# Moving the second group's memory rows and x to later places in the DMA queue of a two-group encoder kernel

## The reference, cut to what matters

```python
def memory_attention(q, mem, mem_norm, w_mem_kv, q_norm, k_norm):
    q = rmsnorm(q.reshape(B, S, MEM_HEADS, MEM_HEAD_DIM), q_norm)
    kv = rmsnorm(mem, mem_norm) @ w_mem_kv      # needs the mean square of each row of mem
    ...
def trunk(x, mem, p):
    for i in range(DEPTH):                      # 2 layers
        h = rmsnorm(x, p['norm_in'][i])
        z = h @ (a_w_in or b_w_in)              # q parts, q_mem, gate
        mix = mla_mixer(...) if i % 2 == 0 else swa_mixer(...)
        mem_o = memory_attention(q_mem, mem, ...)
        branch = concatenate([mix, mem_o]) * silu(gate)
        x = x + branch @ p['w_out'][i]
    return x
y_prompt, y_sample = trunk(x_prompt, mem_prompt, p), trunk(x_sample, mem_sample, p)
```

## Time and profile before

| | before |
|---|---|
| median of three runs | 1411.21 us |
| profiled execution | 1412.02 us, its span 1410.2 us |
| TensorE (PE) busy | 1383.9 us, 98% |
| VectorE (DVE) busy | 972.9 us, 69% |
| ScalarE (ACT) busy | 759.3 us, 54% |
| GpSimd (POOL) busy | 408.4 us, 29% |
| moved by DMA | 122.52 MB, mean 87 GB/s |

### The profile page before, as it was taken

One profiled execution on the slowest core, in us unless ns is written; L12 is line 12 of the kernel. 1 busy time (PEld: TensorE's weight loads), 2 busy tenths in 40 slices (PEclk: granted clock), 3 DMA queues, 4 the chain that ended last, 5 costly groups with the idle time before them and its releaser, 6 DMA issues.

```text
span 1410.2 us, 22918 instructions
## 1 busy us (share of the span) xinstructions
PE 1383.9 (98%) x8072; PEld 1233.9 (87%) x8072; DVE 972.9 (69%) x2035; ACT 759.3 (54%) x1815; POOL 408.4 (29%) x525
## 2 busy tenths in 40 slices
PE   7899999999999999999999999999999999999999
PEld 5688989888888889899888898898888888899997
DVE  6356578888674646898664656878876556488883
ACT  6344466556463535777453544665555445377661
POOL 2032243321021302655212212423302022238450
PEclk9999999999999999999999999999999999999999
DMA  5422221111542132221454132211123412222222
GB/s 212 143 56 73 79 85 44 49 48 35 193 148 79 50 101 78 69 70 56 135 164 131 46 90 79 68 47 44 50 91 115 138 57 71 76 87 68 68 76 105
DMA packets 89825, 122.52 MB, mean 87 GB/s; under 512 B 10480, under 2 KB 58992, under 8 KB 89712
## 3 DMA queue, kind: packets, MB, share of 16 engines
q1 hardware_dynamic: 84240, 113.36, 26.3%
q10 hardware_dynamic: 5472, 7.69, 1.8%
HBM read 116.82 MB, written 4.19 MB: 86 GB/s over the span
## 4 chain that ended last, share of the span: by engine, by line
PE 86%; DVE 5%; ACT 3%; POOL 2%; DMA 2%; issue 2%; SPq 1%; ACTq 0%; DVEq 0%; POOLq 0%
PE bank L1577 25%; PE bank L1579 24%; PE bank L1578 24%; PE bank L1623 8%; PE bank L1583 2%; PE bank L1584 2%; DVE w_lo_t L932 1%; POOL rr L1399 1%; DMA w_raw<-in_w_out 1%; DMA w_raw<-in_w_a 1%; POOL rtmp L1398 1%; ACT w_hi L579 1%; DVE ss L952 1%; ACT q_st L601 0%; DVE cT L942 0%
## 5 line engine op out<-in xcount | busy, mean ns | idle before, releaser
L932 DVE TENSOR_TENSOR w_lo_t<-w_raw,w_hi 128x256 fp32r<-128x256 f32 (+3 forms) x540 | 305.2, 580 | 266.0 <-ACT w_hi L579 252.8
L579 ACT ACTIVATE w_hi<-w_raw 128x256 fp32r<-128x256 f32 (+3 forms) x544 | 268.2, 508 | 336.2 <-PE bank L1579 302.5
L1577 PE MATMUL bank<-w_hi,actT 128*128 128x256 f32 (+3 forms) x1120 | 362.1, 323 | 7.8 <-DVE w_lo_t L932 7.8
L1578 PE MATMUL bank<-w_lo_t,actT 128*128 128x256 f32 (+3 forms) x1120 | 360.0, 321 | 0.0
L1577 PEld LDWEIGHTS bank<-w_hi,actT 128*128 128x128 f32 x1120 | 213.0, 190 | 24.2 <-issue 5.8
L1578 PEld LDWEIGHTS bank<-w_lo_t,actT 128*128 128x128 f32 x1120 | 213.1, 190 | 14.6
L1460 POOL TENSOR_TENSOR prob<-prob,rinv 128x256 f32<-128x256 f32 x192 | 136.4, 740 | 257.6 <-DVE rinv L1038 257.6
L604 ACT ACTIVATE prob<-bank,nmax 128x256 f32<-128x256 f32 (+2 forms) x256 | 138.7, 552 | 106.1 <-DVE nmax L1242 39.7
L1579 PE MATMUL bank<-w_hi,brlo 128*128 128x256 f32 (+1 forms) x608 | 188.9, 311 | 0.0
L1579 PE MATMUL bank<-w_hi,actT 128*128 128x512 f32 (+3 forms) x512 | 170.8, 334 | 0.0
L1577 PE MATMUL bank<-actT,w_hi 128*128 128x512 f32 x384 | 152.5, 397 | 0.0
(11 more groups left out here) (151 smaller groups left out, 2682.7 us busy)
## 6 DMA issues: line engine op xcount, KB each, us to landing
w_raw<-in_w_mem SPq DMA_DIRECT2D x64, 256.0 KB, 2.7
w_raw<-in_w_out SPq DMA_DIRECT2D x112, 128.0 KB, 2.1
w_raw<-in_w_b SPq DMA_DIRECT2D x112, 128.0 KB, 2.1
w_raw<-in_w_b SPq DMA_DIRECT2D x48, 256.0 KB, 2.7
w_raw<-in_w_out SPq DMA_DIRECT2D x40, 256.0 KB, 2.7
w_raw<-in_w_a SPq DMA_DIRECT2D x32, 256.0 KB, 2.7
w_raw<-in_w_a SPq DMA_DIRECT2D x64, 128.0 KB, 2.0
bias<-in_alibi ACTq DMA_DIRECT2D x28, 192.0 KB, 2.3
```

Of the source, the lines that this page charges most:

```text
L579: act.activation(w_hi[:, n % SPLIT, 0:width], w_raw[:, n % RAW, 0:width], ACT.Copy).then_inc(w_hi_done, 1)
L932: dve.tensor_tensor(w_lo_t[:, n % SPLIT, 0:width], w_raw[:, n % RAW, 0:width], w_hi[:, n % SPLIT, 0:width].bitcast(fp32), ALU.subtract).th ...
L1577: nc.tensor.matmul(out, lhs[0], rhs[0], start=start, stop=False, skip_group_check=skip)
L1578: nc.tensor.matmul(out, lhs[0], rhs[1], start=False, stop=False, skip_group_check=skip)
```

## The change

The rows of the second group's memory are no longer loaded ahead of tile 16. They are loaded at the end of layer 0, where x of that group was. `last_squares` and `memory_scales(1)` run in layer 1 instead of layer 0. x of the second group is loaded in layer 1, between tile 163 (the last of `qmem`) and tile 164 (the first of `gate` 8 to 11), still behind the wait on `ssm_ready`.

```diff
@@ block.sync
-                for j in range(NM):
-                    sp.dma_start(last_rows[:, j, :], mem[GROUPS - 1, j * P:(j + 1) * P, :]).then_inc(last_rows_in[j], 16)
                 at = FIRST["qmem", 0, NT - 1]
                 for L in range(LAYERS):
+                    if L % 2 == 1 and L // 2 + 1 < GROUPS:
+                        load_weights(at, FIRST["gate", L, 11])
+                        at = FIRST["gate", L, 11]
+                        load_x(L // 2 + 1)
                     if L + 1 < LAYERS:
                         load_weights(at, FIRST["out", L, 0, NT - 1])
                         at = FIRST["out", L, 0, NT - 1]
                         load_mem(L + 1)
-                    if L % 2 == 0 and L // 2 + 1 < GROUPS:
-                        load_x(L // 2 + 1)
+                    if L == 0:
+                        for j in range(NM):
+                            sp.dma_start(last_rows[:, j, :], mem[GROUPS - 1, j * P:(j + 1) * P, :]).then_inc(last_rows_in[j], 16)
@@ block.scalar
-                    if L == 0:
+                    if L == 1:
                         last_squares()
@@ block.gpsimd
                     batches(MH, MD, NT)
+                    if L == 1:
+                        memory_scales(1)
                     if L == 0:
-                        memory_scales(1)
```

## The result

The changed kernel takes 1400.87 us (median of four runs, 1400.37 to 1402.63), the kernel before 1410.95 us on the same chip: ratio 0.9933, 95% interval 0.9916 to 0.9950, so 7 to 12 us less. Run again later beside the other kernels it took 1401.53 us against 1409.32, ratio 0.9947 (0.9934 to 0.9960). The forecast was 1405.0 with a range of 1401.5 to 1409.5: the direction was right, the gain was larger than forecast and just outside the range.

A forecast was written before the change was run, and what follows sets the result against it. TensorE, busy 98% of the span, was taken as the bound, so only its stalls or low-clock stretches could be given back. -2.6 - 2.3 - 1.3 = -6.2 us gave 1405.0 us against the median, range 1401.5 to 1409.5.

The forecast's parts named there:

- rival F: Further on in the kernel: another wait takes the gain back, counted as no change; chance 0.04.
- Part 3: Layer 1: x ahead of tile 164, the rows' squares and the scales cost 0, with up to 1.4 us kept open.
- rival E: Layer 1: x's 2.1 MB ahead of tile 164 stalls TensorE, net +6.9 us, 1418.1; chance 0.05.
- Part 1: Start of layer 0: without the rows ahead, tile 16's pause falls from 5.4 to 2.75 us, -2.6, and the clock holds, -2.3.
- The clock's term: Behind tile 16's pause in layer 0: TensorE's clock stays at full speed after the shorter pause, -2.3 us.
- rival C: Layer 0: tile 16 lands in time, pause and low clock both go, -9.0 us in all, 1402.2; chance 0.18.
- Rival D: Layer 0: the tables, not the rows, hold the queue ahead of tile 16; only -2.3 us, 1408.9; chance 0.13.
- The rows' term: Ahead of tile 16 in layer 0: removing 1.05 MB of rows at 400 GB/s saves 2.6 us.
- The term of 1.3 at tile 132: End of layer 0, output projection: waits of 1.15 and 0.18 us go, gain 1.3 us, between 0 and 1.3.

The follow-up runs named there:

- x_ahead_of_qmem: Changed kernel with the second group's x issued ahead of tile 156, layer 1's first `qmem` tile, and rows squared earlier: 1411.83 us, ratio 1.0011 to the kernel before.
- rows_stay_tables_later: Kernel before with only the five tables moved from ahead of tile 16 to behind tile 19, rows staying: 1404.69 us against 1409.86, ratio 0.9961.
- rows_behind_16: Kernel before with the two row DMAs issued directly behind tile 16 instead of ahead of it: 1405.23 us against 1410.07, ratio 0.9968.
- tables_behind_19: Changed kernel with the five table loads moved from ahead of tile 16 to behind tile 19: 1400.91 us, ratio 0.9942 to the kernel before.
- rows_eighth: Kernel before with rows moved between tiles 23 and 24, except one eighth (two 64 KB DMAs) left ahead of tile 16: 1403.09 us against 1410.07.
- before_busy_wait: Kernel before with 40 identity transposes on TensorE ahead of its wait for tile 16: 1407.32 us against 1409.86, ratio 0.9982.

## Why the prediction was wrong in size

**The plan of the argument held.** TensorE's waits were the right place to look; the three that the change touches went or shrank to 0.54 us, and nothing took their place (rival F). ScalarE's squares, GpSimd's scales and x in layer 1 cost nothing, as in Part 3. x_ahead_of_qmem shows that rival E was a real danger: x did not stop TensorE ahead of `gate`, where a tile lasts 2.7 us, and did ahead of `qmem`, behind tiles of 1.4 us. Its price was put at 13.1; one chunk earlier, and with the wait for the squares in it, it was 9.0.

**The step that failed** is in Part 1: "I count the issue time at nothing" and "the tile then lands at 45.64 - 2.6 = 43.0". The rows were sized by their bytes alone at 400 GB/s. Measured, the tile lands 4.8 us earlier, not 2.6, so the pause went from 5.37 to 0.54 us and not to 2.75. These are the landings, counted in the kernel before from this line:

```profile
32.34 0.33 SPq L536
```

| ahead of tile 16 | its issue after tile 15's, us | its DMA, us | landing after tile 15's issue, us | TensorE's wait, us |
|---|---|---|---|---|
| tables and rows (before) | 3.69 | 9.61 | 45.64 - 32.34 = 13.3 | 5.37 |
| rows (rows_stay_tables_later) | 2.57 | 6.27 | 41.30 - 32.46 = 8.8 | 0.91 |
| tables (after) | 2.75 | 5.75 | 38.95 - 30.45 = 8.5 | 0.54 |
| tables, rows behind (rows_behind_16) | 2.75 | 6.34 | 41.11 - 32.02 = 9.1 | 1.17 |
| neither (tables_behind_19) | 2.58 | 2.8 | 37.54 - 32.15 = 5.4 | none |

Each line is one profile. With the tables alone the landing is 7.9 to 8.9 us in five of them, with both 12.9 to 13.3 in three, so 4.8 is good to about half a microsecond. The wait is the landing less 7.9 to 8.0 us in each line that has one: by then the tile must be there. Tables alone add 3.1 us, rows alone 3.4, both 7.9, more than their sum. The rows thus cost more behind the tables (4.8) than alone (3.4), and both more than 1.05 / 0.4 = 2.6.

The second and third column say where the sum goes wrong. From its own issue the tile takes 3.0 us longer behind the tables, 3.5 behind the rows and 6.8 behind both, which is nearly the sum. The rest is the issue: tile 16's ring place comes free only 2.6 us after tile 15's issue, and in that time the issues of the tables or those of the rows fit, but not both. So the issues of one of the two cost nothing, and those of the other come on top.
The 4.8 us are thus 0.95 us of earlier issue and 3.9 us of a shorter DMA, and both parts were sized wrong. But it can't be said that issue time as such costs 0.95: rows_eighth has the two issues as well and lands at 8.3. What the profile shows beside it is the start of the stream: with the whole rows in the queue it begins later, 18 GB/s at 36 to 38 us in the earlier trace rows against 95 GB/s already at 34 to 36 us after, 1.9 us being the shift between the two. I had seen the dead time and taken it as given by the tables. Why the stream starts later with the rows in the queue, and why 1.05 MB take over 3 us where 400 GB/s would need 2.6, stays open; rows_eighth says only that it goes with the bytes.

The clock's term came as forecast, 2.3 us, and before_busy_wait gives 2.5. But that was luck in part: it had been put as nearly even for a pause of 2.75 us, and no run has a pause of TensorE between 1.2 and 5.2 us, so whether the clock would have held behind that one stays open.

So rival C, at 0.18, was nearly what happened: -4.83 - 2.3 - 1.33 = -8.5 against its -9.0, with 0.54 us of wait left. Rival D was half right: the tables hold the queue as much as the rows do, but the two had to come together to be felt.

**The range** ended at 1401.5, just above the 1400.87 measured. 8.5 us below the kernel before are 1400.8 to 1402.5 by its five medians (1409.32 to 1410.95), and in the first comparison, whose kernel before took 1410.95, the changed kernel fell 1.6 us lower than 1402.5. The rows' term alone would have left the time inside the range, at its lower end. What put it outside is the spread between executions, and the term for it that I left out is the early or late rise of the clock at the start, 1.9 us between two executions, visible in the first 18 us of the trace, which I had read only for the wait of 9.5 us. The term of 1.3 at tile 132 was right for this trace and at its upper end over several (0.18 to 1.33).

## What to carry to other kernels

A load in a shared DMA queue is free only up to the cover of the tile that is queued behind it. Compute that cover for every place in the queue where a load could stand. Ahead of `qmem` tile 16 had to land 8.0 us after tile 15's issue, which is 5.4 us after its own ring place was free: ring depth times the work of one tile, 4 x 1.36. Of these its own DMA takes 2.8. The same x cost nothing ahead of `gate`, with tiles of 2.7 us in the ring. One chunk earlier, x and the squares that it waits for cost 9 us: what a load waits for holds the whole queue.

Near the edge of the cover, loads must be counted together: each of two alone was almost hidden, and whichever one is moved appears to bring nearly the whole gain. And a pause of TensorE long enough to lower its clock costs more than itself, here 5.4 us and 2.3 more.

## What had not been expected of the hardware

- A tile's landing is not its bytes ahead over the rate: 1.05 MB cost 3.4 us alone and 4.8 us behind 0.33 MB of tables, of which three are in pieces of 64 or 256 B, where 400 GB/s would give 2.6.
- The moment at which TensorE reaches its full pace at the start differs between profiles of the same work, 10 or 18 matmuls in the 4 us from 14 to 18 us. With fourteen transposes of 0.23 us each ahead of the work the spread of five runs was 0.3 us, and 1.9 without them on another chip.
- With two 64 KB DMAs more in the queue a tile landed 8.3 us after its neighbour's issue, inside the 7.9 to 8.9 us of the five profiles without them.
